# A two-block decoder kernel: the second layer's memory set around the state-space end, the post norm by tiles, x turned in pairs

## The reference

```python
def hybrid_layer(x, mem, pre_g, post_g, w_in, ..., mem_norm_g, w_mem_kv, w_out):
    hn = rmsnorm(x, pre_g)
    proj = hn @ w_in
    ...
    y_mem = memory_read(mem_q, rmsnorm(mem, mem_norm_g), w_mem_kv) * silu(mem_g)
    y = concatenate([y_ret, y_ssd, y_sb, y_mem], axis=-1) @ w_out
    return x + rmsnorm(y, post_g)

def memory_read(q, mem_n, w_mem_kv):
    kv = mem_n @ w_mem_kv            # mem is the same in both layers: 256 x 1024
    k, v = split(kv, 2, axis=-1)
    ...
```

## Time and profile before

| | us |
|---|---|
| median of 3 runs | 3189.04 (3185.53 to 3190.9) |
| the profiled execution | 3188.54 |
| its span, first to last instruction | 3186.7 |
| TensorE busy | 2962.8 |
| VectorE busy | 1396.3 |
| ScalarE busy | 991.4 |
| GpSimd busy | 91.2 |
| mean granted TensorE clock | 0.972 of full |

### The profile page before, as it was taken

One profiled execution on the slowest core, in us unless ns is written; L12 is line 12 of the kernel. 1 busy time (PEld: TensorE's weight loads), 2 busy tenths in 40 slices (PEclk: granted clock), 3 DMA queues, 4 the chain that ended last, 5 costly groups with the idle time before them and its releaser, 6 DMA issues.

```text
span 3186.7 us, 33344 instructions
## 1 busy us (share of the span) xinstructions
PE 2962.8 (93%) x14369; PEld 2443.4 (77%) x14369; DVE 1396.3 (44%) x1924; ACT 991.4 (31%) x1234; POOL 91.2 (3%) x96
## 2 busy tenths in 40 slices
PE   6999998589999987999998899999999998899997
PEld 5878777478877766888885688888888886588886
DVE  4345246733532665333364443334433354544234
ACT  3322332233133222212354342224222253442122
POOL 0010000100100001000100000000000010000000
PEclk9999999799999988999999899999999999999999
DMA  5221111222121202232431123222232251123322
GB/s 189 68 96 68 66 67 53 70 93 68 65 93 40 89 31 100 93 106 93 114 88 52 53 93 118 94 93 96 103 117 96 100 100 66 56 91 106 106 93 79
DMA packets 40659, 275.84 MB, mean 87 GB/s; under 512 B 5492, under 2 KB 5682, under 8 KB 8768
## 3 DMA queue, kind: packets, MB, share of 16 engines
q1 hardware_dynamic: 35136, 253.77, 23.5%
q0 software_dynamic: 4560, 16.27, 2.3%
q10 hardware_dynamic: 816, 3.67, 0.3%
HBM read 269.50 MB, written 2.10 MB: 85 GB/s over the span
## 4 chain that ended last, share of the span: by engine, by line
PE 84%; DVE 10%; ACT 4%; issue 1%; DMA 0%; ACTq 0%; DVEq 0%; POOLq 0%
PE G L355 14%; PE G L356 14%; PE G L357 14%; PE G L367 11%; PE G L369 10%; PE G L368 10%; DVE w_lo L1286 2%; PE A L600 1%; ACT w_hi L911 1%; PE A L839 1%; PE A L501 1%; PE A L817 1%; PE A L827 1%; ACT work L1235 1%; PE A L615 1%
## 5 line engine op out<-in xcount | busy, mean ns | idle before, releaser
L1286 DVE TENSOR_TENSOR w_lo<-raw,w_hi 128x2048 fp32r<-128x2048 f32 x236 | 536.3, 2273 | 856.0 <-ACT w_hi L911 855.0
L355 PE MATMUL G<-xT_hi,w_hi 128*128 128x512 f32 (+1 forms) x2272 | 867.4, 382 | 27.8 <-DVE xT_lo L1327 8.5
L356 PE MATMUL G<-xT_lo,w_hi 128*128 128x512 f32 (+1 forms) x2272 | 857.1, 377 | 0.0
L357 PE MATMUL G<-xT_hi,w_lo 128*128 128x512 f32 (+1 forms) x2272 | 857.1, 377 | 0.0
L911 ACT ACTIVATE w_hi<-raw 128x2048 fp32r<-128x2048 f32 x236 | 447.1, 1896 | 972.4 <-PE G L369 513.7
L355 PEld LDWEIGHTS G<-xT_hi,w_hi 128*128 128x128 f32 x2272 | 432.5, 190 | 122.0 <-issue 20.8
L357 PEld LDWEIGHTS G<-xT_hi,w_lo 128*128 128x128 f32 x2272 | 432.4, 190 | 77.5
L356 PEld LDWEIGHTS G<-xT_lo,w_hi 128*128 128x128 f32 x2272 | 432.8, 191 | 74.2
L367 PE MATMUL G<-w_hi,h_hi 128*128 128x512 f32 x704 | 274.7, 390 | 0.0
L369 PE MATMUL G<-w_hi,h_lo 128*128 128x512 f32 x704 | 274.1, 389 | 0.0
L368 PE MATMUL G<-w_lo,h_hi 128*128 128x512 f32 x704 | 274.0, 389 | 0.0
(11 more groups left out here) (270 smaller groups left out, 3003.6 us busy)
## 6 DMA issues: line engine op xcount, KB each, us to landing
raw<-in_stream SPq DMA_DIRECT2D x240, 1024.0 KB, 4.8
lnr<-in_ln_rows POOLq DMA_DIRECT2D x6, 1024.0 KB, 5.3
row<-in_rows POOLq DMA_DIRECT2D x6, 512.0 KB, 7.9
fA<-in_mem POOLq DMA_DIRECT2D x2, 1024.0 KB, 7.5
x<-in_x ACTq DMA_DIRECT2D x1, 2048.0 KB, 10.4
out<-x SPq DMA_DIRECT2D x4, 512.0 KB, 2.6
shift_t<-work POOLq DMA_DIRECT2D x32, 62.0 KB, 14.5
cst<-in_const ACTq DMA_DIRECT2D x1, 1474.0 KB, 13.6
```

The source lines that it names most:

```text
L355: mm(o, a, hi[:, c, at:at + n], start=start and own_start, stop=False, **k)
L356: mm(o, a, lo[:, c, at:at + n], start=False, stop=False, **k)
L357: return mm(o, wl[:, col:col + P], hi[:, c, at:at + n], start=False, stop=stop, **k)
L1286: tt(w_lo[:, s, 0:nk, :], raw[:, r, 0:nk, :], w_hi[:, s, 0:nk, :].bitcast(F32), ALU.subtract).then_inc(lo_done, 1)
```

## The change

It does the following.

- The second layer's memory: loaded into `mem_s` (a view of `sA`) after the third state product of the first layer's state-space part; squared by ScalarE (`mem_sq`), normed by VectorE within the last chunk; turned into columns 256 to 511 of `xT`; keys are made ahead of `last_out` (`memory_keys`), values behind it (`memory_values`), in which the first two tiles of x are turned after six of eight steps. The weight stream's order follows. Keys go to `tB` instead of `y_acc`.
- The post norm works by tiles: ScalarE squares `y_acc` and, for the next layer, x; VectorE multiplies by the gain (`weighed`), adds to x in one pass (`x_sum`), and norms (`x_norm`). GpSimd adds nothing.
- x is turned in pairs of tiles, and the product behind it (the first product of x in both layers, the first of the second block) is made in token halves (`tile_halves`); the second pair is turned within the first half.
- Gains are loaded earlier on GpSimd's queue, and the loads of function tables ahead of these roots are gone.

```diff
@@ -286,7 +291,13 @@
...
-            order = [l * BLOCK1 + i for l in range(DEPTH) for i in READ1]
+            order = []
+            for l in range(DEPTH):
+                last = l + 1 == DEPTH
+                keys, values = ([], []) if last else ([(l + 1) * BLOCK1 + i for i in READ1[0:2]],
+                                                      [(l + 1) * BLOCK1 + i for i in READ1[2:4]])
+                order += [l * BLOCK1 + i for i in READ1[4 if l else 0:36]] + keys
+                order += [l * BLOCK1 + i for i in READ1[36:38]] + values
...
@@ -453,9 +464,48 @@
...
-                                turn_normed(L, 1)
...
+            def feature_halves():
+
+                return [[(o, [feat(o, xT_hi, xT_lo, o * P, 256, 256 * p, p == 0)]) for o in range(4)] for p in range(2)]
...
+            def token_pair(tile, pair):
+
+                transposes(lambda t: tile(2 * pair + t), 2, 2)
...
+            def tile_halves(tile):
+
+                base = N.tr - 4
+
+                def ready(p, b):
+                    pe.wait_ge(S["tr_lo"], base + 4 * p + 3 + b)
+                gemm_token_halves(feature_halves(), ready, lambda: token_pair(tile, 1))
...
+            def memory_keys(read=lambda: None):
+
+                transposes(lambda t: xn[:, 0, :], 1, 2)
+                read()
+                transposes(lambda t: xn[:, 1, :], 1, 2)
+                pe.wait_ge(S["tr_lo"], N.tr)
+                feat4(N_MEM, 256)
...
+            def memory_values():
+
+                steps = gemm_steps((4, 4), [(o, [tok(o, xT_hi, xT_lo, 2 + o // 2, col=(o % 2) * 256, n=256)])
+                                            for o in range(4)])
+                advance(steps, 6)
+                token_pair(x_tile, 0)
+                advance(steps, 2)
+                finished(steps)
...
@@ -706,14 +756,12 @@
...
-                Pos.pair, Pos.off, Pos.ubase, Pos.u = l * (BLOCK1 // 2), 0, l * UNITS1, 0
-                transposes(lambda t: xn[:, t, :], 2, 2)
-                pe.wait_ge(S["tr_lo"], N.tr)
-                feat4(N_MEM)
-                gemm((4, 4), [(o, [tok(o, xT_hi, xT_lo, o // 2, col=(o % 2) * 256, n=256)]) for o in range(4)])
-                transposes(lambda t: xn[:, t, :] if t < 2 else mem_t[:, t - 2, :], 4, 2)
-                pe.wait_ge(S["tr_lo"], N.tr)
-                feat4()
+                more = l + 1 < DEPTH
+                Pos.pair, Pos.off, Pos.ubase, Pos.u = l * (BLOCK1 // 2), 4 if l else 0, l * UNITS1, 2 if l else 0
+                if l == 0:
+                    memory_keys()
+                    memory_values()
+                tile_halves(x_tile)
...
@@ -725,12 +773,12 @@
...
+                if more:
+                    memory_keys(lambda: pe.wait_ge(S["d_yu"], so_far(l, "d_yu") + 4))
                 last_out()
...
+                if more:
+                    memory_values()
...
@@ -1126,12 +1181,68 @@
...
-                rsqrt(8)
-                tr_hi(mixT_hi, TILES, 1)
+                if more:
+                    param(act, l + 1, "mem_in")
+                    for t in range(2):
+                        fn(xn[:, t, :], mem_s[:, t, :], ACT.Square, accum_out=rs_v[:, 8 + t:9 + t]).then_inc(S["mem_sq"], 1)
+                    rsqrt(2, 8, preload=False)
+                    tr_hi(xT_hi, 2, 2, 2)
+                    rsqrt(8, preload=False)
+                    split()
+                    keys()
+                    next_unit(1)
+                    tr_hi(mixT_hi, 2, 1)
+                    split()
+                    tr_hi(mixT_hi, 2, 1, 2)
+                else:
+                    rsqrt(8, preload=False)
+                    tr_hi(mixT_hi, TILES, 1)
                 next_unit(1)
-                next_unit(0)
-                rsqrt(4)
...
+                def square_y(t):
+                    if t:
+                        act.wait_ge(S["y_sq"], so_far(l, "y_sq") + t)
+                    if t == 3 and more:
+                        act.wait_ge(S["x_sq"], so_far(l, "x_sq") + 2)
+                    act.wait_ge(g_free[t], Pos.ubase + Pos.u + 2)
+                    fn(junk, y_acc[:, t, :], ACT.Square, accum_out=rs_v[:, 10 + t:11 + t]).then_inc(S["y_sq"], 1)
+
+                def square_x(t):
+                    act.wait_ge(S["y_sq"], so_far(l, "y_sq") + (3 if t < 2 else 4))
+                    if t:
+                        act.wait_ge(S["x_sq"], so_far(l, "x_sq") + t)
+                    act.wait_ge(S["x_added"], so_far(l, "x_added") + t + 1)
+                    fn(junk, x[:, t, :], ACT.Square, accum_out=rs_v[:, t:t + 1]).then_inc(S["x_sq"], 1)
+                split()
+                square_y(0)
+                square_y(1)
+                rsqrt(2, 10, preload=False)
+                square_y(2)
+                if more:
+                    split()
+                    square_x(0)
+                    square_x(1)
+                    rsqrt(2, 0, preload=False)
+                    square_y(3)
+                    rsqrt(2, 12, preload=False)
+                    next_unit(2)
+                    split()
+                    tr_hi(xT_hi, 2, 2)
+                    values()
+                    next_unit(2)
+                    split()
+                    square_x(2)
+                    square_x(3)
+                    rsqrt(2, 2, preload=False)
+                    tr_hi(xT_hi, 2, 2, 2)
+                else:
+                    tr_hi(xT_hi, 2, 2)
+                    square_y(3)
+                    rsqrt(2, 12, preload=False)
+                    split()
+                    next_unit(0)
...
@@ -1420,24 +1524,108 @@
...
+            def mean_square(name, count, n, at):
+
+                dve.wait_ge(S[name], so_far(l, name) + count)
+                ts(rs_v[:, at:at + n], rs_v[:, at:at + n], 1.0 / D, EPS, ALU.mult, ALU.add).then_inc(S["rs_in"], 1)
+
+            def added(t):
+
+                done(t)
+                o = y_acc[:, t, 512:1024]
+                tt(o, o, G[:, t, :], ALU.add).then_inc(g_free[t], 1)
+
+            def weighed(t):
+
+                dve.wait_ge(g_free[t], Pos.ubase + Pos.u + 2)
+                tt(mem_t[:, t % 2, :], y_acc[:, t, :], row[:, POST_G:POST_G + D], ALU.mult).then_inc(S["y_scaled"], 1)
+
+            def x_sum(t):
+
+                dve.wait_ge(S["y_scaled"], so_far(l, "y_scaled") + t + 1)
+                stt(out=x[:, t, :], in0=mem_t[:, t % 2, :], scalar=rs_r[:, 10 + t:11 + t], in1=x[:, t, :],
+                    op0=ALU.mult, op1=ALU.add).then_inc(S["x_added"], 1)
+
+            def x_norm(t):
+
+                dve.wait_ge(S["x_added"], so_far(l, "x_added") + t + 1)
+                stt(out=x_tile(t), in0=x[:, t, :], scalar=rs_r[:, t:t + 1], in1=row[:, PRE_G:PRE_G + D],
+                    op0=ALU.mult, op1=ALU.mult).then_inc(S["tr_src"], 1)
+
+            def pair_summed(pair):
+
+                dve.wait_ge(S["x_added"], so_far(l, "x_added") + 2 * pair + 2)
...
             def last_out(finish):
 
-                for t in range(TILES):
-                    finish(t)
-                    if t:
-                        low(t - 1)
-                low(TILES - 1)
+                if more:
+                    for t in range(TILES):
+                        finish(t)
+                    split()
+                    next_unit(1)
+                    low(0)
+                    low(1)
+                    split()
+                    low(2)
+                    low(3)
+                else:
+                    for t in range(TILES):
+                        finish(t)
+                        if t:
+                            low(t - 1)
+                    low(TILES - 1)
                 add_out(0)
                 next_unit(1)
-                for b in range(4):
-                    done(b)
-                    o = y_acc[:, b, 512:1024]
-                    tt(o, o, G[:, b, :], ALU.add).then_inc(g_free[b], 1)
-                    dve.wait_ge(g_free[b], Pos.ubase + Pos.u + 2)
-                    link(nc.vector.tensor_tensor_reduce(
-                        out=xn[:, 0, :], in0=y_acc[:, b, :], in1=y_acc[:, b, :], scale=1.0, scalar=0.0,
-                        op0=ALU.mult, op1=ALU.add, accum_out=rs_v[:, b:b + 1]))
-                next_unit(0)
+                split()
+                added(0)
+                added(1)
+                weighed(0)
+                weighed(1)
+                mean_square("y_sq", 2, 2, 10)
+                added(2)
+                newton(2, 10)
+                x_sum(0)
+                x_sum(1)
+                if more:
+                    split()
+                    added(3)
+                    dve.wait_ge(S["x_added"], so_far(l, "x_added") + 2)
+                    weighed(2)
+                    weighed(3)
+                    mean_square("x_sq", 2, 2, 0)
+                    mean_square("y_sq", 4, 2, 12)
+                    param(dve, l + 1, "pre_g_in")
+                    newton(2, 0)
+                    x_norm(0)
+                    x_norm(1)
+                    next_unit(2)
```

(68 more changed lines are left out.)

113 lines of the change are left out of this document (62 added, 51 removed).

## The result

The changed kernel takes 3129.78 us (median of 4 runs, 3128.51 to 3139.02), the kernel before beside it 3187.61 (4 runs, 3185.53 to 3190.90). The ratio is 0.9824, with the interval 0.9803 to 0.9845.

The account below looks back on a forecast made before the run. TensorE, busy 93% of the span, was taken to bound the kernel, so only its waits and low clock could pay. Gains 34.9 + 11.8 less a loss of 4.0 make 42.7: 3189 - 43 = 3146 us, range 3136 to 3162.

Parts of the forecast that it names:

- The passage to the second layer: From the state-space part's end to the end of the second layer's first product: a gain of 34.9 us, ends 26 and 38.
- The rival of table loads: Squares need another function table; some five switches per passage take 12 us of the gain: 3158, chance 0.07.
- The start of the first layer: Up to the end of x's first product there: later turned pieces and a longer wait lose 4.0 us, ends 1.5 and 5.
- The 2.5 for the clock: Start of the first layer: 2.5 us more for matmuls at the lower clock behind a TensorE wait of 6.6.
- The passage to the second block: From the last output product's end to the end of the second block's first product: gain 11.8 us, ends 8 and 13.5.
- The waits came out as listed: Sign to look for: TensorE's waits in front of the second block are near 2, 1.7 and under 1 us.
- part of its matmuls at the low clock: Second block's first product, half 0: 26 matmuls of its block 0 at 0.21 us, ending at 1220.1; passage ends 1239.3, otherwise 1238.2.
- Later work is paced by TensorE and moves up by as much.: Work behind the three places keeps its length, so the whole kernel gains their sum, 42.7 us.
- the rival "better": Whole kernel: the clock never falls and nothing meets badly, a gain of 50 us: 3139, chance 0.10.
- The slower rival: The clock stays at 1.2 GHz through the passages, costing 98 us more: 3244, chance 0.04.

Follow-up runs that it names:

- b_delay3: The kernel before, with three writes of zeros on VectorE ahead of the last addition to x before the second block: 3188.87 us, ratio to before 0.9997.
- b_vector_adds: The kernel before, with all four additions of y to x on VectorE and none on GpSimd: 3175.41 us, ratio to before 0.9958.
- a_delay2: The changed kernel, with two writes of zeros on VectorE ahead of the release of x's first pair for the second block: 3132.52 us, ratio to before 0.9823.
- b_shift: The kernel before, with two writes of zeros into y_acc on VectorE at the program's start: 3188.07 us, ratio to before 0.9996.

## Why the prediction was right in part and missed the time

**The passage to the second layer: right.** Its 34.9 was built step by step, and the trace has the steps, shifted by the 2.36 us that the first layer ended later: keys at 574.2 + 2.36 = 576.56 (576.55), `last_out` done by 615.4 (614.5), x turned at 626.9 (626.00), the halves at 632.2 (631.15). The differences are two terms. Keys were given 13.7 for a part at the low clock and took 13.0 (576.55 to 589.54), and the stall behind them was 0.97, not 1.1. The 36.2 itself hangs in part on the execution: the same code of before took 128.54 from the first matmul of L687 to the memory attention pass in its own trace and 125.79 in b_delay3's, which differs from it only later. The gain has three carriers, each measured by undoing it: the halves 12.5, the keys' place 7.3, GpSimd's additions 1.9 (by b_vector_adds, in the old order). If these add up, the remainder, about 14.5, is left to the norm by tiles and the values beside it; no run has it alone. They need not add up: at the second block the halves (12.7) and GpSimd's additions (1.9) come to more than the 13.8 of both together.

**The rival of table loads: wrong.** No load stands beside the squares. They took 1.04 to 1.06 each with 0.19 for the sum, 1.14 from start to end in the rows below, where 1.2 was taken:

```profile
563.49 1.04 ACT L1187 ACTIVATE xn<-sA 128x1024 f32<-128x1024 f32 x1
564.44 0.19 ACT L1187 ACTIVATION_READ_ACCUMULATOR xn<-sA 128x1 f32 x1
```

**The start of the first layer: mechanism right, size too large.** The product started at 62.47, predicted 62.4, behind a wait of 6.44, predicted 6.6. From there the clock was low (0.64 from 62.47 to 66.47) as foreseen. The loss was 2.55 between these two traces, not 4.0, and 1.6 between the means of five traces each; both lie inside the ends of 1.5 and 5. The 2.5 for the clock were read off a pause of 7.85 and were the mis-sized term.

**The passage to the second block: 13.8 instead of 11.8, just over the upper end of 13.5.** The waits came out as listed (1.62, 1.73, 0.39). I had given the first half part of its matmuls at the low clock; it ran at 0.99:

```profile
1150.00:1224.00 74.00, 70.07 (x417) 61.66 (x415) 37.01 (x46) 25.45 (x35) 5.88 (x7) 0.99 0.31 108
```

By the rule of the Trainium skill that the prediction weighed ("TensorE: Matmul & The Clock Gate", Part 4), each half behind transposes would have started at 1.2 GHz. The trace disagrees here as well: over 1172 to 1176, with transposes and no other matmuls, the granted clock was 1.00. It did fall in a_delay2, where these transposes stood behind a wait of 3.92 us and not of 1.62.

```profile
1172.00:1176.00 4.00, 1.94 (x16) 1.73 (x16) 3.85 (x6) 2.71 (x5) 0.00 (x0) 1.00 0.00 0
```

The clearer case is the one in the earlier trace rows, where 32 transposes followed the wait of 15.12 and no other matmul ran before 1229.34. The clock rose while they ran, in the trace of before:

```profile
1221.40:1226.90 5.50, 5.50 (x26) 5.50 (x27) 5.15 (x6) 3.16 (x6) 5.49 (x7) 0.50 0.77 271
1227.00:1229.30 2.30, 0.76 (x7) 0.52 (x5) 2.13 (x5) 1.42 (x3) 0.27 (x1) 1.00 1.03 342
```

**The step that failed: "Later work is paced by TensorE and moves up by as much."** It moves up, but it does not keep its speed. The sum treated the second block as a fixed length, and its length hangs on where the clock changes: the neighbourhood attention alone took 41.96 or 50.96 us with the same instructions. The kernel before stood on the slow one in nearly every execution, which makes it look like a property of its code; the changed kernel stood on the fast one in at least three of four (3128.5 to 3130.3; the fourth, 3139.02, has the distance of the fall, but no trace). Without this term the sum would have been 60.0 - 10.1 = 49.9 of gain, or 3139, in the range and at the place of the rival "better". The other 7.2 us of the miss are small and spread over five stretches, each predicted 0.9 to 2.0 too low; alone they would have stayed inside the range. I had looked at the clock only where the change removes a wait, and listed the falls of the passages; the page of before gives no sign that the longest fall of the second block depends on its start. The slower rival (the clock stays down through the passages) had the right cause, the clock, in the wrong place and with the wrong sign.

About 10 of the 58 us are therefore not owed to less work or fewer waits. One write of zeros gets 9.0 of them in the kernel before (7.3 in the median, since the write itself costs), and a reordering worth 1 us loses them in the changed one.

**What stays open.** The runs show that the moment decides, and that delays between 1.2 and 3.6 us pass through both cases. Why the kernel before met the bad case in almost every execution is shown in part. Its program starts at any place against the clock's moments: TensorE's first matmul lies 0.30 to 2.98 us behind one in the five traces with its code up to the second passage (before, the three with delays, and b_shift but for its writes). At 1135 us the same five lie 0.28 to 0.56 us behind one. So on the way the program falls into step with the clock, and comes to this wait at nearly the same place each time. Which waits do that was not taken apart. Nor does any run show why a moment 1.62 to 1.71 us behind the wait brings the fall and one 1.85 us behind it does not.

## What to carry to other kernels

When two versions differ by under 1% and TensorE's clock falls anywhere in stretches of small matmuls, compare the granted clock stage by stage before crediting the edit, and add a delay of 1 to 3 us to both as a control: a gain that a useless instruction can give or take is not the edit's. Halves of a product that let its operand come in pairs are worth their longer matmul time (23.0 against 21.8) where they fill a wait of 8 us or more, as they did twice here (8.70 and 11.42); at the first layer, where 4.9 us of wait were to be filled, they cost more than they brought. An independent product set into a wait gives no more than that wait is long: the wait was 8.0 us, and the keys' place was worth 7.3 of their 13.

## What the runs showed of the hardware

- The same 199 matmuls, with one wait of 1.9 us among them, ran in 41.96 or 50.96 us. With the clock fallen to 0.5 it stayed there over some 24 us, although TensorE was busy for 20.96 of 24.50; moved by 1.2 us, the same instructions took 41.95 us at 0.99. In sixteen traces this fall came exactly where a change moment of the clock lay 1.62 to 1.71 us behind the wait.
- GpSimd's additions of 128x1024 slowed VectorE's multiplications beside them from 1.28 to 2.26 us in the mean (9.05 for four), and took 3.25 to 3.32 each themselves; four on VectorE take 1.22 each.
- A squaring with its sum on ScalarE (128x1024) took 1.04 to 1.06 plus 0.19 and needed no table load between exponentials.
- The clock kept 1.00 over 4 us in which TensorE did nothing but 16 transposes, behind a wait of 1.62 us. In the trace of before it rose from 0.50 to 1.00 at about 1227 us, while the 32 transposes from 1221.34 to 1227.76 ran.
